# A two-block transformer kernel on one core: a strip split ahead of the sources behind it, sums of squares multiplied two units later, and strips split in halves inside two attentions

## What is computed

```python
# first block, layers l = 0 and 1; width of the tokens 512 + 256 in layer 0, 512 in layer 1
h = h + mx[5] * conv_ffn(modulate(rmsnorm(h, norm2_g[l]), mx[3], mx[4]), w_up[l], conv_w[l], conv_b[l], w_down[l])
# end of the first block, start of the second
x = rmsnorm(h, final_g)
h = _rms(x, mix_norm_g)                    # two norms in a row, both from sums over h
p = h @ w_in
# second block: latent attention (8 heads of 96), later memory attention (4 heads of 256)
s = (einsum('bqhd,bkhd->bhqk', qn, k_nope) + einsum('bqhr,bkr->bhqk', qr, k_rot)) * scale
o = einsum('bhqk,bkhd->bqhd', softmax(s), v)
```

## Time and profile before

| | |
|---|---|
| median of 3 runs | 2773.83 us (2773.24 to 2775.17) |
| profiled execution, its own time | 2779.62 us |
| its span, first to last instruction | 2777.8 us |
| busy: PE, DVE, ACT, POOL | 2487.8 (90%), 1375.2 (50%), 868.5 (31%), 251.7 (9%) |
| mean granted clock of PE | 0.949 of full speed |
| a strip of 704 KB, from issue to landing | 4.0 us |
| first down projection, matmuls from | 893.05 us |
| expert stage, 2540 to 2720 us | DMA busy share 1.01 to 1.02 |

### The profile page before, as it was taken

The page is one execution under the profiler, slowest core; times in us unless marked ns, Lnnn a source line. Parts: engine busy times, 40 slices in busy tenths (PEclk is TensorE's granted clock), DMA queues, the critical chain, the costliest instruction groups (busy, mean ns, idle before and its releaser), DMA issues. The chain is left out here.

```text
span 2777.8 us, 34833 instructions
## 1 busy us (share of the span) xinstructions
PE 2487.8 (90%) x14602; PEld 1933.5 (70%) x14602; DVE 1375.2 (50%) x2185; ACT 868.5 (31%) x1385; POOL 251.7 (9%) x183
## 2 busy tenths in 40 slices
PE   7997988999998998997889999998977889898976
PEld 5885657888887787995669998764733368573322
DVE  4324554566667214325647777347565645423213
ACT  3222433332324113223444334233424642311001
POOL 0002520000000000003500000000042020011112
PEclk9998989999999999997989999999988999988999
DMA  5114731111111112115612223320201013348997
GB/s 240 61 54 106 269 128 46 46 61 61 63 69 38 53 63 82 61 69 142 224 46 92 92 92 117 111 82 31 87 0 54 0 61 137 121 188 326 421 421 292
DMA packets 58555, 326.88 MB, mean 118 GB/s; under 512 B 8157, under 2 KB 14429, under 8 KB 26461
## 3 DMA queue, kind: packets, MB, share of 16 engines
q1 hardware_dynamic: 45358, 302.76, 29.4%
q0 software_dynamic: 5696, 12.59, 1.2%
q10 hardware_dynamic: 7344, 9.28, 1.0%
HBM read 317.26 MB, written 12.58 MB: 119 GB/s over the span
## 5 line engine op out<-in xcount | busy, mean ns | idle before, releaser
L953 PE MATMUL ps<-work_rounded,ring_rounded 128*128 128x512 f32 (+1 forms) x2016 | 537.0, 354 | 19.1 <-DVE work_rounded L397 10.6
L953 PE MATMUL ps<-xn_rounded,ring_rounded 128*128 128x512 f32 (+2 forms) x2304 | 541.8, 347 | 0.0
L2003 PE MATMUL ps<-xn_rounded,ring_rounded 128*128 128x258 f32 (+2 forms) x2816 | 535.1, 312 | 0.0
L2003 PEld LDWEIGHTS ps<-xn_rounded,ring_rounded 128*128 128x128 f32 x2816 | 414.6, 191 | 31.2
L953 PEld LDWEIGHTS ps<-xn_rounded,ring_rounded 128*128 128x128 f32 x2304 | 373.4, 191 | 57.6 <-issue 0.2
L953 PEld LDWEIGHTS ps<-work_rounded,ring_rounded 128*128 128x128 f32 x2016 | 336.5, 192 | 76.3 <-DVE work_rounded L397 11.8
L953 PE MATMUL ps<-big_rounded,ring_rounded 128*128 128x512 f32 (+1 forms) x1200 | 326.3, 364 | 45.0 <-DVE big_rounded L859 25.0
L859 DVE TENSOR_TENSOR ring_rounded<-ring,ring_rounded 128x2048 fp32r<-128x2048 f32 (+2 forms) x94 | 189.1, 2015 | 266.5 <-ACT ring_rounded L824 266.5
L2003 PE MATMUL ps<-work_rounded,ring_rounded 128*128 128x256 f32 (+1 forms) x1232 | 280.2, 309 | 9.0 <-PEq L784 4.8
L953 PEld LDWEIGHTS ps<-big_rounded,ring_rounded 128*128 128x128 f32 x1200 | 203.4, 196 | 84.8 <-DVE ring_rounded L859 21.4
L824 ACT ACTIVATE ring_rounded<-ring 128x2048 fp32r<-128x2048 f32 (+2 forms) x94 | 158.2, 1687 | 314.7 <-PE ps L953 298.3
(11 more groups left out here) (420 smaller groups left out, 3125.4 us busy)
## 6 DMA issues: line engine op xcount, KB each, us to landing
ring<-in_stream SPq DMA_DIRECT2D x141, 1024.0 KB, 4.8
big<-in_experts SPq DMA_DIRECT2D x44, 1024.0 KB, 26.0
ring<-in_stream SPq DMA_DIRECT2D x32, 704.0 KB, 4.0
ring<-in_experts SPq DMA_DIRECT2D x22, 1024.0 KB, 27.3
xn<-in_experts SPq DMA_DIRECT2D x15, 1024.0 KB, 28.4
work<-in_experts SPq DMA_DIRECT2D x15, 1024.0 KB, 28.7
big<-in_first_modulation SPq DMA_DIRECT2D x8, 1024.0 KB, 14.1
work<-in_bias ACTq DMA_DIRECT2D x24, 256.0 KB, 3.9
```

The source lines that it names most:

```text
L953: mm = pe.matmul(out[:, a - u.first:b - u.first], lhs, rhs, start=j == 0 and n == 0 and not u.onto, stop=j == terms - 1 and n == len(passe ...
L2003: mm = pe.matmul(out[:, a:b], ws[:, k, :], x[k][:, a - base:b - base], start=k == 0 and n == 0, stop=k == KT - 1 and n == 2)
```

## The change

Three places.

1. Both down projections pass `early`: the second strip is split ahead of source tile 8 in layer 0 (no strip or tile is split ahead there, so behind eight tiles) and ahead of tile 10 in layer 1 (behind the one tile 9).
2. `PairNorm.before` multiplies the sums of squares by ones ahead of unit 4, no longer ahead of unit 2.
3. In the attentions each of the two strips is split in two halves of 1024 columns: ACT after its work of units 4, 6, 8 and 10, DVE after its of units 5, 7, 9 and 11. `strip_high` counts halves.

```diff
@@ PairNorm.before
-        if i == 2:
+        if i == 4:
             pe.wait_ge(b.sig("squares_added").sem, b.sig("squares_added").at(2 * KT - 2))
@@ attention, vector
+                def halves_low(part):
+                    for _, value, high in views[part // 2:part // 2 + 1]:
+                        r = slice(part % 2 * 1024, part % 2 * 1024 + value.shape[1] // 2)
+                        dve.wait_ge(strip_high.sem, strip_high.at(part + 1))
+                        self.split_low(dve, value[:, r], high[:, r])
...
-                    if u == 5:
-                        self.low_ahead(dve, views)
+                    if u in (5, 7, 9, 11):
+                        halves_low((u - 5) // 2)
@@ attention, scalar
+                def halves_high(part):
+                    for n, value, high in views[part // 2:part // 2 + 1]:
+                        r = slice(part % 2 * 1024, part % 2 * 1024 + value.shape[1] // 2)
+                        self.strip(act, n)
+                        self.split_high(act, value[:, r], high[:, r]).then_inc(strip_high.up(), 1)
...
-                    if u == 4:
-                        self.high_ahead(act, views)
+                    if u in (4, 6, 8, 10):
+                        halves_high((u - 4) // 2)
@@ ffn_down
-        self.project(units, 2 * KT, finish, banks_each=2, sources=sources, tiles_ahead=tiles_ahead,
+        self.project(units, 2 * KT, finish, banks_each=2, sources=sources, tiles_ahead=tiles_ahead, early=10 if last else 8,
```

More of the change, by code:

```diff
@@ L1058, in attention @@
         views = self.split_ahead(ahead)
-        next_high = self.sig("next_high")
+        next_high, strip_high = self.sig("next_high"), self.sig("strip_high")
+        assert all(value.shape[1] == STRIP for _, value, _ in views)
         def pair_at(u, place):
```

## The result

| | before | changed |
|---|---|---|
| median of 16 runs each, us | 2775.43 (2773.24 to 2780.50) | 2780.69 (2771.98 to 2791.36) |
| profiled execution, its own time and its span | 2779.62, 2777.8 | 2778.69, 2776.8 |
| busy: PE, DVE, ACT | 2487.8, 1375.2, 868.5 | 2484.9, 1376.1, 868.9 |
| mean granted clock of PE | 0.949 | 0.950 |

The account below looks back on a forecast made before the run. PE, busy 90% of the span, was taken as the bound. The terms -8.4 + 0 + 8.8 + 0.6 - 1.6 + 0 + 1.8 = +1.2, on the median of 2773.8, gave 2775.0, range 2770 to 2781.

Parts of the forecast that it names:

- 8.4: First down projection, layer 0: gain from the early second strip, 5.8 of idle and 2.6 of lower clock.
- rival C: Layer 0: second strip not landed at its pass, or tiles late; gain 0, 2783; chance 0.05.
- bounds of -0.4 to +0.3: Second down projection, layer 1: range around a forecast effect of 0 from the early strip.
- 9.4: Second projection: loss from the later sums of squares, 8.8 for the chain and 0.6 for the clock.
- rival B: Second projection: ones matmuls don't bind, the chain stays hidden; -2.3 in place of +9.4, 2763; chance 0.04.
- The clock term: Second projection, unit 4: lower clock lasting longer after some 15 us idle; 0.6, bounds nothing and 2.6.
- The 8.8: Second projection: loss as the ones matmuls come later and their chain to unit 4 is no longer hidden.
- The walk: Both attentions: queues followed unit by unit with halved strips; gain 1.6 in the latent attention, 0 in the memory attention.
- The gain of 1.6: Latent attention: gain from strips in halves, 1.4 of it the lower clock after 6.01 idle.
- The memory attention's +1.8: Memory attention: clock loss from one wait ahead of the values, half of eight matmuls at half the clock; bounds 0 and 4.
- Rival A: Attentions' short waits each cost clock, four more at 1.5, plus the full 2.6 in the second projection; 2783; chance 0.11.
- +1.2: Whole kernel: sum of all forecast terms, taken as no change.

Follow-up runs that it names:

- e7: Kernel before with the ones matmuls ahead of unit 4 and the third strip split ahead of the wait for the sums: 2776.21 for 2777.22, ratio 0.9994.
- e2: Kernel before with only the sums of squares multiplied ahead of unit 4: 2786.20, ratio 1.0044.
- e4: The whole change without the halves in the attentions, against the kernel before: 2777.14, ratio 1.0017.
- six turns: Kernel before with each attention run six times in a row, strips in halves against whole splits: 3486.22 for 3474.37.
- e3: Kernel before with only the strips of both attentions split in halves: 2778.68, ratio 1.0007.
- f2: The changed kernel run once more, unaltered, for a third trace: traced execution 2789.98.
- e8: Kernel before with early down strips, ones ahead of unit 3 behind the third strip's split, attention halves back to back during value matmuls: 2751.22 for 2777.22, ratio 0.9908.
- e1: Kernel before with only the early second strip of the down projections: 2771.02 for 2776.84, ratio 0.9989.

## Why the forecast failed, step by step

**First down projection: right.** 8.4 was forecast; up to unit 1 it is 33.85 - 25.63 = 8.2. Over all traces the stage means 759.8 in nine with the part and 768.1 in six without, 8.3. The idle of 5.70 is gone and its lower clock too, tiles 8 to 21 came in time (rival C is out), and the later strips weren't late.

**Second down projection: 0 in most executions, 1.2 in some.** In twelve traces it lasts 128.34 to 128.72 whether the part is in or not. In executions with the quick start PE wants tile 11 sooner, and there PE waits 1.02 to 1.08 for the strip; the early strip takes that away, 127.2 to 127.4 for 128.4. The bounds of -0.4 to +0.3 rested on one trace, in which the start was slow.

**Second projection: right in mechanism, 0.5 short, by two errors.** 9.4 was forecast, 9.9 measured. The idle is the 15 of the forecast, and e7 shows the queue behind the evictions to be the whole reason (rival B is out). The clock term, 0.6 after the longer idle, measured 0: from unit 4 on nothing changed. The 8.8 measured 10. It rested on units 2 and 3 starting 2.30 earlier, the idle of before's one trace. But that idle is what DVE's sums leave of PE's start: the ones stand 15.02 to 15.05 after the stage's start in every trace with the old order, with 2.39 to 0.87 idle ahead of them. This is the row of the down part alone:

```profile
1904.22 1.12 PE L533 MATMUL ps<-xn,base 128*128 128x512 f32 x2 [0.90 <-DVE xn L547]
```

What shortens the idle is the lower clock at the stage's start (from 2 to 6 us after it the granted clock is 0.87 in before, 0.50 in the down part alone), which had been hidden behind that wait. With the ones moved nothing hides it: they come 25.0 to 25.1 after the start (changed kernel, e2, e4) or, in the two traces at 2790, 23.8. So the move costs 10.0 or 8.8, by the clock at the start. In the mean over all traces of either order the stage is 111.8 for 102.3, 9.4 longer; that this is the forecast's figure is chance, as its two errors cancel there.

**Attentions: here the working failed.** The walk itself holds: units 6, 8 and 10 of the latent attention stand within 0.1 of it. The price of the waits was wrong. "The waits of 2.0 in the latent attention I take as harmless" is the failing sentence: they have a granted clock of 0.72 and 0.50 behind them, and the one of 2.00 costs 1.7 up to unit 12 (36.34 - 34.66), the whole gain. The gain of 1.6 shrank to 0.4 in the mean of six turns, and in the whole kernel to nothing (+0.1). The memory attention's +1.8 was about right: 2.3 in the mean of six turns, 1.4 in the whole kernel's traces; the wait ahead of the values costs 1.69 in the changed kernel's trace, as forecast, and nothing in e3 and f2. Together +1.9 in the turns and +1.5 in the whole kernel, not +0.2. Rival A had the mechanism, but not each short wait brings the clock down, and it asked 1.8 + 6 = 7.8; measured in the turns are 1.2 in the latent and 2.3 in the memory attention, 0.4 for each of eight waits in the mean. The Trainium skill, "TensorE: Matmul & The Clock Gate", section on oscillation, describes that loop for a kernel whose waits are longer than these. The traces agree with it only in part: the clock fell behind waits of 1.89, 2.00, 2.41 and 2.92, and in two traces behind 0.81, and didn't behind others of 1.87 and 2.41.

**What the sum left out.** With these sizes it is -8.3 + 9.9 - 0.4 + 2.3 = +3.5, and +3.1 with the attentions as in the whole kernel. The lower ten of the 16 times have a median of 2778.6, +3.2. The other 2.1 of the 5.3 are the upper group. The failing premise is "All other stages keep their instructions ... so what a stage gains or loses moves all that follows": a stage with the same instructions doesn't have the same time when it falls on the lower clock, and the filter tables did so in a third of the traces with the down part, for 11.4 us. By that share it takes 3 to 4 of the down part's 8.3 in the mean; its own times fit (-3.1 by the ratio, while its lower eight have a median 7.4 under before's). No row of before could have priced it, and why the clock stays low there is open.

The forecast of no change thus rested on a sum, +1.2, 2.3 under what the parts gave in the traces, and on the premise that the clock would treat all else alike. Errors of 1 to 2 us each had one direction; two large terms of opposite sign left no margin for them.

## What to carry to other kernels

A pass that holds up PE isn't made harmless by cutting it into pieces spread over as many units: each piece makes a short wait, and behind some of these waits the clock falls. Put the pass undivided, or its halves one behind the other, where PE has work of its own (9.3 of e8's 26 us are from the two attentions, with the same passes). When a step of a norm is moved later, look at what is queued behind its last wait; moving that ahead made the difference between +10 and -0.5. And where large terms cancel, the small clock terms decide, so give them both their bounds rather than their likeliest values.

## What the hardware showed that was not expected

- Granted clock after short waits of PE: 0.72 and 0.50 after 1.89 and 2.00 in the latent attention, while 2.30 in the second projection cost nothing. In one trace of the memory attention the clock fell behind one wait of 2.41 and not behind another; behind the same wait of 0.81 the last values took 5.40 in two traces and 3.70 in the others.
- One unchanged stage ran 11.44 us longer, 27 us of it at 0.50 with PE busy throughout, behind a barrier idle of 1.18 that is the same in the executions in which the clock stays at 1.00. In the three traces that have it, the stage ahead was 1.2 shorter than otherwise.
- Such patterns repeat: the kernels e1 and e4, which are alike up to the second projection, agree to 0.22 in each of the twelve stages before it in their traces, and the long stage was 63.35 in three traces on two chips.
